# A two-block transformer kernel on one core: x loaded first, two output panels rounded in GLA, bias DMA later, self-attention's tail reordered

## The reference

```python
# first block; m0 to m8 are modulation vectors, silu(c) @ ada_w + ada_b
x   = x + 0.5 * m2 * swiglu(modulate(rms_norm(x), m0, m1), ffn1)      # the same for ctx
y   = token_mixing(norm 2 of x and ctx)        # x @ w_in, then
      # retention: 4 heads of 128, chunks of 128, both directions
      # GLA: 4 heads of dk 64 and dv 128, gated, chunks of 64, both directions
      # per-head norms, times silu(gate), concatenated, @ w_out
x   = x + m5 * y
x   = rms_norm(x + 0.5 * m8 * swiglu(modulate(rms_norm(x), m6, m7), ffn2))
# second block
proj = rmsnorm(h) @ w_in_2                     # q, k, v (8 heads of 64), u, y
attn = dilated_mixture_attention(rope(q), rope(k), v)
rec  = bidirectional_rglru(conv(u)) * gelu(y)  # 512 wide
h = h + concatenate([attn, rec]) @ w_out_2
h = h + memory_cross_attention(rmsnorm(h), rmsnorm(mem))   # 256 memory rows
h = h + square(relu(rmsnorm(h) @ w_mlp_in)) @ w_mlp_out    # 4096 wide
return rmsnorm(h)
```

## Time and profile before

| what | value |
|---|---|
| median of three runs | 2064.55 us (2061.88 to 2066.39) |
| the profiled execution, its time | 2061.67 us |
| its span, first to last instruction | 2059.9 us |
| TensorE busy with products | 1948.4 us, 95% of the span |
| TensorE's weight loads, beside them | 1631.1 us, 79% |
| VectorE busy | 1038.9 us, 50% |
| ScalarE busy | 834.6 us, 41% |
| GpSimd busy | 838.0 us, 41% |
| moved by DMA | 197.66 MB, 96 GB/s mean |
| TensorE's mean granted clock | 0.973 of full speed |

### The profile page before, as it was taken

How to read it: one execution, slowest core, us unless ns; L and a number is a source line. 1 busy time by engine, 2 the same in 40 slices (tenths; PEclk the granted TensorE clock), 3 DMA queues, 4 the chain that set the end, 5 groups by cost and what they waited for, 6 DMA issues and landing times.

```text
span 2059.9 us, 25718 instructions
## 1 busy us (share of the span) xinstructions
PE 1948.4 (95%) x9378; PEld 1631.1 (79%) x9378; DVE 1038.9 (50%) x1563; ACT 834.6 (41%) x1276; POOL 838.0 (41%) x414
## 2 busy tenths in 40 slices
PE   4999999999989999888999999999888989999998
PEld 2999999999978875556788888877745767888886
DVE  4879877567456225954313112577985353121123
ACT  4425243334354135652442224437555454232231
POOL 1347565556324321523344454433522324443432
PEclk8999999999999999889999999999989999999999
DMA  8134343443212120003222332332311212232321
GB/s 348 59 126 142 129 160 117 150 148 120 91 62 82 61 71 31 11 1 107 82 92 91 102 106 86 104 113 76 107 63 42 82 42 85 98 112 82 112 82 61
DMA packets 53486, 197.66 MB, mean 96 GB/s; under 512 B 6320, under 2 KB 7056, under 8 KB 51600
## 3 DMA queue, kind: packets, MB, share of 16 engines
q1 hardware_dynamic: 52240, 191.47, 27.4%
q10 hardware_dynamic: 1152, 4.92, 0.7%
HBM read 194.27 MB, written 2.10 MB: 95 GB/s over the span
## 4 chain that ended last, share of the span: by engine, by line
PE 60%; issue 17%; DVE 10%; POOL 6%; ACT 4%; DMA 2%; SPq 0%; POOLq 0%; DVEq 0%; ACTq 0%
PE ps L2271 27%; PE ps L2400 13%; PE ps L2437 8%; POOL wlo L649 6%; PE ps L2285 2%; DMA ada_f<-ada_p 1%; PE ps L2626 1%; PE ps L2258 1%; PE ps L2259 1%; PE ps L2260 1%; PE ps L2698 1%; PE ps L2617 1%; PE ps L2774 1%; DVE ada_prod L1408 1%; PE ps L2799 1%
## 5 line engine op out<-in xcount | busy, mean ns | idle before, releaser
L649 POOL TENSOR_TENSOR wlo<-raw,whi 128x1024 fp32r<-128x1024 f32 x244 | 604.5, 2488 | 997.6 <-ACT whi L702 973.6
L702 ACT ACTIVATE whi<-raw 128x1024 fp32r<-128x1024 f32 x244 | 253.4, 1053 | 289.8 <-PE ps L2271 198.1
L2271 PE MATMUL ps<-h_hi,whi 128*128 128x512 f32 (+2 forms) x992 | 362.2, 379 | 4.3 <-DVE act_a L1565 1.7
L2271 PE MATMUL ps<-h_hi,wlo 128*128 128x512 f32 (+2 forms) x992 | 359.6, 377 | 0.0
L2271 PE MATMUL ps<-h_lo,whi 128*128 128x512 f32 (+2 forms) x992 | 359.0, 376 | 0.0
L2271 PEld LDWEIGHTS ps<-h_hi,whi 128*128 128x128 f32 x992 | 182.7, 188 | 43.0 <-issue 8.1
L656 POOL TENSOR_TENSOR wlo<-raw,whi 128x512 fp32r<-128x512 f32 x108 | 160.3, 1498 | 136.5 <-ACT whi L870 136.1
L2271 PEld LDWEIGHTS ps<-h_lo,whi 128*128 128x128 f32 x992 | 182.3, 188 | 33.4 <-issue 1.0
L2271 PEld LDWEIGHTS ps<-h_hi,wlo 128*128 128x128 f32 x992 | 182.5, 188 | 32.6
L2271 PE MATMUL ps<-g_hi,whi 128*128 128x512 f32 x432 | 168.0, 389 | 0.0
L2271 PE MATMUL ps<-g_lo,whi 128*128 128x512 f32 x432 | 168.0, 389 | 0.0
(11 more groups left out here) (464 smaller groups left out, 3683.0 us busy)
## 6 DMA issues: line engine op xcount, KB each, us to landing
raw<-panels SPq DMA_DIRECT2D x280, 512.0 KB, 3.7
ada_w<-ada_t SPq DMA_DIRECT2D x56, 512.0 KB, 4.1
ada_f<-ada_p SPq DMA_DIRECT2D x8, 1024.0 KB, 19.0
x_lat<-x_t SPq DMA_DIRECT2D x1, 2048.0 KB, 8.1
out<-x_lat SPq DMA_DIRECT2D x8, 256.0 KB, 2.2
x_ctx<-ctx_t SPq DMA_DIRECT2D x1, 1024.0 KB, 10.2
cond_b<-cond SPq DMA_DIRECT2D x1, 1024.0 KB, 21.8
x_ctx<-mem_t ACTq DMA_DIRECT2D x1, 1024.0 KB, 4.8
```

Source lines behind the costliest of these rows:

```text
L649: pool.tensor_tensor(wlo[:, sl], raw[:, sl], whi[:, sl].bitcast(f32), ALU.subtract).then_inc(lo_done, 1)
L702: act.activation(whi[:, sl], raw[:, sl], ACT.Copy).then_inc(hi_done, 1)
L2271: ins = pe.matmul(bank(banks + b, n), wt[:, w], a[:, at_(kc, c0):at_(kc, c0) + n], start=kc == 0 and j == 0, stop=kc == n_k - 1 and j == 2)
```

## The change

It has five parts; none adds or drops a product, a rounding or a byte.

- x and the context are issued ahead of the eight small transfers.
- In the first layer VectorE's last `first_output` moves ahead of the `ada_chunk` that stood before it, and `first_output` first waits until the earlier output's subtraction (`g_ready`) is done.
- Output panels 2 and 3 are rounded in GLA's second pair, behind levels 7 and 8, and `outputs_and_squares(..., rounded=2)` skips them. GpSimd's program stays as it is.
- The wait for the fourth recurrence group, and the bias DMA with it, move from n = 17 to n = 19 of the second input projection.
- In self-attention's tail TensorE's values of pair 2 are interleaved with the last four transposed items. The recurrence half of output panel 0 (`recurrent_part`) follows, then the values of pair 3, then the attention half (`attention_part`). ScalarE's `merged` of pair 2 moves behind its last `transposed`. Panels 1 to 3 are written out, and the loop in `residual` starts at its second round.

```diff
--- before.py
+++ after.py
@@ -555,6 +555,8 @@
 
         @block.sync
         def _(sp):
+            sp.dma_start(x_lat[:, :], x_t).then_inc(x_loaded, 16)
+            sp.dma_start(x_ctx[:, :], ctx_t).then_inc(x_loaded, 16)
             sp.dma_start(vec[:, :], vecs).then_inc(vec_loaded, 16)
             sp.dma_start(cond_s[:, :], cond_t).then_inc(condt_loaded, 16)
             sp.dma_start(lsig[:, 0:8], decays.partition_broadcast(P)).then_inc(small_loaded, 16)
@@ -563,8 +565,6 @@
                 sp.dma_start(gate_sb[d][:, :], gate_w[:, d * 256:(d + 1) * 256]).then_inc(small_loaded, 16)
             sp.dma_start(ident[:, :], ident_h).then_inc(small_loaded, 16)
             sp.dma_start(rope_pp[:, :], rope_pp_h).then_inc(small_loaded, 16)
-            sp.dma_start(x_lat[:, :], x_t).then_inc(x_loaded, 16)
-            sp.dma_start(x_ctx[:, :], ctx_t).then_inc(x_loaded, 16)
             for kc in range(KC):
                 if kc == KC - 2:
                     for s in range(2):
@@ -945,7 +945,7 @@
                     for c in range(RING):
                         round_ahead(G["p_down"], i, c)
 
-            def outputs_and_squares(p0, m):
+            def outputs_and_squares(p0, m, rounded=0):
 
                 def follow(o):
                     if m.late or m.n == 3:
@@ -954,7 +954,7 @@
 
                 for o in range(KC):
                     q = p0 + o + 2
-                    if q < N_PANELS:
+                    if rounded <= o and q < N_PANELS:
                         round_panel(q % RING, q // RING + 1, q - RING)
                     if o >= 2:
                         follow(o - 2)
@@ -1122,6 +1122,9 @@
                         pair_root(0)
                     if u == 6:
                         spread_copy()
+                    if u in (7, 8):
+                        q = P_WOUT + u - 5
+                        round_panel(q % RING, q // RING + 1, q - RING)
                 pair_hi(0)
                 pair_out(1)
                 pair_root(1)
@@ -1215,7 +1218,7 @@
                         round_for(P_WIN2, P_WOUT2, first, n_p)
                     if n == 0:
                         mix_root()
-                    if n == 17:
+                    if n == 19:
                         act.wait_ge(rg_hid, 4)
                         act.dma_start(bias_sb[:, :], window_bias).then_inc(bias_loaded, 16)
                     act.wait_ge(panel_done, done(P_WIN2 + first + n_p - 1))
@@ -1307,8 +1310,9 @@
                         if m % 8 == 0 and m >= 16:
                             act.wait_ge(a_values, m // 4 - 2)
                         transposed(SELF, m)
-                        if m % 8 == 5 and m > 8:
+                        if m % 8 == 5 and 8 < m < 24:
                             merged(SELF, m // 8 - 1)
+                merged(SELF, HEADS - 2)
                 merged(SELF, HEADS - 1)
 
             def cross_attention():
@@ -1357,7 +1361,7 @@
             act.wait_ge(o_ready, 2 * HEADS)
             act.dma_start(x_ctx[:, :], mem_t).then_inc(mem_loaded, 16)
             act.dma_start(pos_i[:, :], positions.partition_broadcast(P)).then_inc(pos_loaded, 16)
-            outputs_and_squares(P_WOUT, norms[2])
+            outputs_and_squares(P_WOUT, norms[2], rounded=2)
             norm(norms[2])
             for G in GROUPS[0:3]:
                 hidden_up(G)
@@ -1592,6 +1596,7 @@
 
                 dve.wait_ge(panel_done, done(2 * f + 1))
                 dve.wait_ge(silu_done, f + 1)
+                dve.wait_ge(g_ready, f + 2)
                 dve.tensor_tensor(columns_of(prod, 0, TOK), columns_of(act_a, 0, TOK), outputs(4 * (f % 2) + 2, TOK), ALU.mult).then_inc(up_evac, 1)
                 dve.wait_ge(ghi_done, f + 1)
                 sl = slice(f * TOK, (f + 1) * TOK)
@@ -1703,8 +1708,8 @@
                 ada_chunk(a + 4)
                 first_output(2)
                 token_low(3)
+                first_output(3)
                 ada_chunk(a + 5)
-                first_output(3)
                 ada_chunk(a + 6)
                 ada_chunk(a + 7)
                 dve.wait_ge(ada_used, ada_rows(24))
@@ -2788,17 +2793,19 @@
 
                 pe.wait_ge(win2_evac, len(WIN2) - 1)
 
-                def values(j):
-                    if j >= 2:
-                        pe.wait_ge(mix_ready, SELF["s0"] + j - 1)
-                    pe.wait_ge(a_copied, 8 * (j + 1))
-                    for t in range(LT):
+                def values(j, t0=0, t1=LT):
+                    if t0 == 0:
+                        if j >= 2:
+                            pe.wait_ge(mix_ready, SELF["s0"] + j - 1)
+                        pe.wait_ge(a_copied, 8 * (j + 1))
+                    for t in range(t0, t1):
                         for e in range(2):
                             r = slice(64 * e, 64 * e + 64)
                             v = av[:, t * 512 + (2 * j + e) * DH:t * 512 + (2 * j + e + 1) * DH]
                             ins = pe.matmul(ps[r, (4 + j % 2) * 512:(5 + j % 2) * 512], v, prob_cols(SELF, 2 * j + e)[:, t * LAT:(t + 1) * LAT],
                                             start=t == 0, stop=t == LT - 1)
-                    ins.then_inc(a_values, 2)
+                    if t1 == LT:
+                        ins.then_inc(a_values, 2)
 
                 for g in range(SELF["n"] // GROUP + 2):
                     if g < SELF["n"] // GROUP:
@@ -2809,8 +2816,31 @@
                     if 1 <= g <= SELF["n"] // GROUP:
                         for m in range(GROUP * (g - 1), GROUP * g):
                             transposes(SELF, m)
-                    if g >= 3 and g % 2:
+                            if m >= SELF["n"] - GROUP:
+                                values(HEADS - 2, m - SELF["n"] + GROUP, m - SELF["n"] + GROUP + 1)
+                    if g >= 3 and g % 2 and g != 7:
+                        if g == 9:
+                            recurrent_part()
                         values((g - 3) // 2)
+
+            def recurrent_part():
+
+                pe.wait_ge(lo_done, P_WOUT2 + 1)
+                pe.wait_ge(mix_ready, SELF["s0"])
+                pe.wait_ge(a_max, SELF["n"])
+                for kc in range(4, KC):
+                    w = slice(kc * P, (kc + 1) * P)
+                    for j, (wt, a) in enumerate(((whi, o_hi), (whi, o_lo), (wlo, o_hi))):
+                        pe.matmul(bank(0), wt[:, w], a[:, merged_at(kc, 0):merged_at(kc, LAT)], start=kc == 4 and j == 0, stop=False)
+
+            def attention_part():
+
+                for kc in range(4):
+                    pe.wait_ge(mix_ready, SELF["s0"] + kc + 1)
+                    w = slice(kc * P, (kc + 1) * P)
+                    for j, (wt, a) in enumerate(((whi, o_hi), (whi, o_lo), (wlo, o_hi))):
+                        ins = pe.matmul(bank(0), wt[:, w], a[:, merged_at(kc, 0):merged_at(kc, LAT)], start=False, stop=kc == 3 and j == 2)
+                ins.then_inc(panel_done, 1)
 
             def cross_attention():
 
@@ -2901,7 +2931,11 @@
                     memory_stats()
             input_projection2()
             self_attention()
-            residual(P_WOUT2, L1_OUTS + 4 * KC, o_hi, o_lo, KC, lambda kc: (mix_ready, min(13 + kc, 16)))
+            attention_part()
+            for c in range(1, RING):
+                pe.wait_ge(lo_done, P_WOUT2 + c + 1)
+                panel_product(c, 2 * c, o_hi, o_lo, token_cols(LAT), at_=merged_at).then_inc(panel_done, 1)
+            residual(P_WOUT2, L1_OUTS + 4 * KC, o_hi, o_lo, KC, None, first=1)
             cross_queries()
             cross_attention()
             cross_output()
```

## The result

The change takes **2053.51 us** (median of five runs, 2052.74 to 2053.71) against 2064.55 (2061.88 to 2066.39, five runs in this comparison), a ratio of 0.9947 with a 95% interval of 0.9936 to 0.9958: 11.0 us faster. Forecast were 7.4 us, 2057.2 in a range of 2050.5 to 2062.0. The profiled execution of the change took 2053.71 us, 8.0 less than the profiled one before.

The account below looks back on a forecast made before the run. TensorE was taken to wait for few things, each an isolated stall. Start 0, first layer +0.2, GLA -9.6, bias +2.2 and tail -0.2 summed to -7.4 us: 2057.2 us as a median, range 2050.5 to 2062.

Parts of the forecast that it names:

- its own mechanism: Whole kernel: the forecast's own account of the five parts, -7.4 us together; 2054.5 to 2060 by the bounds, chance 0.48.
- GLA, -9.6: End of GLA: early rounding of output panels 2 and 3 removes TensorE's stall; -9.6 us, between -8.5 and -9.9.
- 7.5 and 2.2: End of GLA: 7.5 us of TensorE stall and 2.2 us of slow clock behind it, both to go.
- x first, 0: Start: x issued earlier, but log sigmoids wait for small transfers behind it; 0 us, between -1.5 and +1.
- the 2.7 us for the rest behind x: Start: estimated time for the small transfers behind x, putting them in at 14.1.
- First layer, +0.2: First layer: stall moves from low part to VectorE's addition, -1.4 and +1.6 for clock; +0.2 us, between -1.5 and +0.7.
- Bias, +2.2: Second input projection: VectorE's products meet GpSimd's subtractions, last key product later; +2.2 us, between -4 and +4.1.
- Self-attention tail, -0.2: Self-attention tail: same products in another order, only waits can go; -0.2 us, between -1.4 and +0.5.
- 1 (bias pays): Second input projection: key products end 2 to 4 us earlier, term -3 instead of +2.2; 2052, chance 0.17.
- 4 (GLA's wait moves on): GLA: the wait moves to output panels 4 to 7, gating products cost 2.3; +4.5 us, 2069, chance 0.05.
- Of 2: Start and first layer: matrices come 1.5 us earlier, clock doesn't fall; -3 us together, 2054, chance 0.14.
- Of 3: Early edits and bias cost more: start +1, first layer +0.7, bias +4.1, GLA -9.0, tail 0; 2061.4, chance 0.16.

Follow-up runs that it names:

- e10: The change with x's start and the bias DMA put back as in the kernel before, interleaved tail kept: 2056.51 us.
- e7: The change, but the values of pair 2 stand as one block ahead of the last 16 transposes: 2054.07 us.
- e11: The change with start and bias DMA as in the kernel before and the values of pair 2 as one block: 2052.01 us.
- e12: The change with the values of pair 2 as one block and the bias DMA back at n = 17, x still first: 2052.84 us.

## Why the prediction was right, and where it wasn't

The sum was -7.4 against -8.0 between the two traces and -11.0 between the medians. In direction and size it held because GLA is most of it. In the change's trace start, first layer and tail each lie outside their own bounds, and with cross-attention, which wasn't forecast, their errors of +1.6, -2.2, +2.2 and -1.7 cancelled: that the small terms add up is luck. The median, 2053.51, lies in the range but below the 2054.5 to 2060 that the forecast gave its own mechanism, between rivals 1 and 2.

- **GLA, -9.6**: the trace gives -9.7, with each intermediate as forecast (no wait, panel 4 in time, gating products covered); the forecast's own terms, 7.5 and 2.2, add up to 9.7. For the piece that was reckoned, the stop and the slow products behind it, the edit is worth 9.3 us; over the whole stage 8.6, since five of six traces without it ran the piece ahead of the stop 0.9 to 1.5 us faster than the one it was taken from.
- **x first, 0**: failed, +1.6 in the trace, about +1.2 over the traces. The step at fault is the 2.7 us for the rest behind x: x and the context were in at 11.19 (forecast 11.4), but the eight small transfers landed one by one up to 15.82, 4.6 us behind them. Each figure behind it came 1.6 to 1.8 late (22.95 for 21.2, 30.2 for 28.5, 40.3 for 38.7). The chain itself was right.
- **First layer, +0.2**: right in mechanism, and in the mean over the traces right in the 1.4 up to the additions. The change's own trace gains 2.0 there, and it doesn't pay the price of the clock, +1.6, which five of eight traces pay: its stall was 3.15 us where 4.5 were forecast.
- **Bias, +2.2**: right in mechanism: the group's products at 2.7 us each, ScalarE's wait ending 4.1 later (1483.17, which is 1493.3 less the 10.1 won before), no wait at panel 24. The size was too high: the last key product, for which +2.2 was forecast, came 1.4 later, because the last rotation gave back 2.7 of the 4.1 us (its middle product took 0.69 for 2.76, the one ahead of it 0.69 for 1.27), where the forecast had 1.9. The +0.5 at self-attention's first items, which makes the trace's 1.9, isn't the edit's: seven of the nine traces without it lose 0.8 to 1.1 there. The edit costs 1.4 us at the last key product and 1.0 at the fifth item.
- **Self-attention tail, -0.2**: failed, +2.0. "TensorE's work from 1564.74 on is unchanged, so only its waits can go" left out three things: that the block of values covers ScalarE's last exponentials, so that the waits stay (1.11 us in e10 for 1.18), that the interleaved products take 0.9 us longer, and that in three of four traces the clock falls. Already the end of pair 2's values, forecast at 1571.5, comes at 1572.3 in e10 (1564.96 plus the 7.34 by which that trace is ahead). The recurrence half ahead of pair 3 is a gain: with the block the tail is 0.9 us shorter than before (e7, e11, e12).
- **Not forecast**: cross-attention, -1.7 in the trace, which the change doesn't touch, and the 2.9 us by which the profiled execution of before lay below its median. The forecast added these 2.9 to both kernels; the change's runs lie within 1.0 us of its trace. Why its five executions agree so well while those of the other kernels spread over 1.8 to 6.8 us, and the 62 of before over 7.4, stays open, and with it some 3 of the 11 us: the parts alone sum to -7.0 in their medians (-8.0, +0.7, +0.6, +0.5, -0.9).
- **Rivals**: 1 (bias pays) and 4 (GLA's wait moves on) have no row. Of 2, the clock that doesn't fall in the first layer came true in the change's own trace, the earlier matrices didn't (the first was in at 18.04, 17.61 before). Of 3, the cost of the start came true. The tail's loss of 2.0 us stands in no rival.

## What to carry to other kernels

When an edit takes independent work away from a place, ask which other engine it was covering there: the block of values looked like an ordinary product and hid the last exponentials. And before a term of one or two microseconds is taken from a trace, take a second trace of the same kernel: here stages with the same code differed by 1.7 us, about as much as each of the four smaller parts was worth.
